# One core, two transformer blocks in fp32: hand-over between projections in units of two k-tiles, one chain for two norms, context rows made between matmul steps

## The chip, the cores and the metric

The kernel runs on one core of one Trainium2 chip. The metric is device microseconds of one execution; the median of three runs is given. The engines are PE (TensorE), ACT (ScalarE), DVE (VectorE), POOL (GpSimd) and SP (SyncE), each with an instruction queue of its own; SP and POOL issue the large transfers. Semaphores order them: an engine that waits holds back everything behind in its queue.

## The reference

256 tokens of width 2048 go through two blocks. Block one: RMS norm, input projection (2048 to 4368), sliding-window attention with sinks and forgetting attention (16 heads each), a norm of each half, output projection; then `x = x + rmsnorm(mix)`, norm, up projection (2 x 5632), a causal depthwise convolution of width 3, `gelu(gate) * val`, down projection, `x = x + rmsnorm(y)`. Block two gets x and a context of 256 rows. Its modulation columns come from `silu(c) @ w_ada + b_ada`.

```
h  = modulate(rms_norm(x, norm_attn_w), sh_a, sc_a)
hc = modulate(rms_norm(ctx, norm_attn_w), csh_a, csc_a)
q, k, v, u = split_projection(h @ w_in); qc, kc, vc, uc = split_projection(hc @ w_in)
x = x + g_a * (concat([attn, pool]) @ w_out)
x = x + g_m * squared_relu_mlp(modulate(rms_norm(x, norm_mlp_w), sh_m, sc_m), w_up, w_down)
return rms_norm(x, final_norm_w)
```

## The kernel before

**Steps.** Every projection is cut into chunks of 512 output columns, and a chunk into steps of two k-tiles (8 steps for a depth of 2048, 6 for the shorter third group of the down projection). fp32 weights and activations are each split into a high part (fp32r) and a low part; PE computes high x high, low x high, high x low for two token blocks and two k-tiles, so a step is 12 matmuls of 128x512 (L1362 to L1364). SP loads raw weights into four slots of two steps. For each step ACT copies `raw` to `w_hi` (`hi`, L541) and DVE subtracts to `w_lo` (`lo`, L837). There are four w buffers, and `hi(s)` waits until step s-4 is done:

```
if s >= 4:
    act.wait_ge(step_done, s - 3 + d)
```

The bodies of a chunk starting at step s prepare the weights of steps s+3 to s+10, so of the next projection the first three steps' weights are ready when a projection ends; the fourth step's come first in ACT's and DVE's next body.

**Projections in order** (names of the code): in1 (9 chunks), attention, out1 (4), up1a/down1a, up1b/down1b, up1c/down1c, in2 (5 chunks, of which the third runs for x and for the context, H + A), attention, pooling and a small mixing matmul (`pool_w`), out2 (4), mlp2 (4 groups of 4 up and 4 down chunks).

**Preparing activations** (`prep` on ACT and DVE, `turn_prep` on PE). Between projections the rows are normalized, transposed and split. Before, this goes in four groups of four k-tiles. PE transposes 8 blocks of 128x128 into two banks of T (L1396). ACT and DVE each take two of the four k-tiles through gain and shift into `u_buf` or `conv` (L521 or L523; L904 or L906). ACT copies 1024 columns to `h_hi` (L531), and DVE subtracts for `h_lo` (L913). All transposes stand ahead of the first step in PE's queue. `h_ready` counts finished groups, and a step waits for its own. The rows are scaled by ACT (token block 0, L502) and DVE (block 1, L886) in pieces of 512 columns.

**Norms.** ACT squares with a running sum (L491), DVE reduces, ACT takes the square root (L497), DVE the reciprocal (L880). After down1c: y2's norm, then x is updated (L1080), then squared, then in2's norm.

**Context.** POOL loads the context into y when in2's activations are ready (L447). ACT squares it after chunk 0 of in2, and the whole preparation stands between chunk 1 and chunk 2.

**Modulation work.** In the gaps of DVE run `ada` operations on tiles of `w_ada` (512 KB each, two buffers) that POOL loads (L402); `ADA_RUNS` is the table of which run does which tiles. A run's loads stand in POOL's queue among its other work: the row for the output scaling (L418), x loaded again (L436, 2 MB), memset of y (L438, L464).

Of the kernel before, what the change touches and what calls it, by code (L numbers as in the profile page):

```python
# [105 lines left out]
def build(nc, a):  # L106
# [173 lines left out]
    PREP = {"in1": (0, 4), "out1": (4, 4), "up1": (8, 4), "in2": (12, 4), "ctx": (16, 4), "out2": (20, 2), "up2": (22, 4)}  # L280
    NORMED = {"out1": 0, "in2": 4, "ctx": 8, "up2": 12}
    X_NEW = {"up1": 0, "in2": 4, "out2": 8, "final": 12}
    STAT = {"in1": 0, "out1": 1, "y1": 2, "up1": 3, "y2": 4, "in2": 5, "ctx": 6, "up2": 7, "final": 8}

    SQUARED = {"in1": 8, "out1": 16, "y1": 24, "up1": 32, "y2": 40, "in2": 48, "ctx": 56, "up2": 64, "final": 72}

    def pipeline(n, pre, gain, fin):

        for t in range(n + 2):
            if t < n and pre:  # L290
                pre(t)
            if 1 <= t <= n:
                gain(t - 1)
            if t >= 2:
                fin(t - 2)
# [1448 lines left out]
```

## Time and profile before

| | us |
|---|---|
| median of three runs (2282.51 to 2287.75) | 2283.95 |
| the profiled execution's own time | 2282.68 |
| its span, first to last instruction | 2281.0 |
| PE busy (share of the span) | 2179.1 (96%) |
| DVE busy | 1526.8 (67%) |
| ACT busy | 1066.0 (47%) |
| POOL busy | 125.7 (6%) |
| mean granted PE clock, 1 is full | 0.976 |

PE is busy nearly always; a share of idle time is not seen in an average, so the places where one projection hands over to the next have to be looked at one by one. Matmuls overlap and their ends are modelled: the time of a step is read from start to start.

### The profile page before, as it was taken

Reading aid. Unit: us, or ns where it says so; the run is one execution under the profiler, and the core shown is the slowest. Engines: PE = TensorE matmul, PEld = TensorE weight load, DVE = VectorE, ACT = ScalarE, POOL = GpSimd, SP = SyncE. Lnnn points to the kernel's source line nnn. Section 1 sums busy time; section 2 is a strip of 40 time slices with the busy share of each in tenths; the row PEclk is TensorE's granted clock in tenths of the full one; section 3 lists DMA queues with packets and bytes.
Section 4 is the critical chain, followed back from the end, with each engine's and each line's share of the span. In section 5 each row is a group of like instructions: output and inputs, shape, how many; then the busy total and the mean of one; then the engine's idle time right before and its main releaser. Section 6 shows DMA issues by size and latency. Waiting matters only on the chain.

```text
span 2281.0 us, 30329 instructions
## 1 busy us (share of the span) xinstructions
PE 2179.1 (96%) x10231; PEld 1803.7 (79%) x10231; DVE 1526.8 (67%) x1841; ACT 1066.0 (47%) x1375; POOL 125.7 (6%) x220
## 2 busy tenths in 40 slices
PE   7999988899999999999978999889999999999997
PEld 5888777788878888888867777777888888888876
DVE  6887778688885787767765364556655555655655
ACT  5444654555433554345456355345434434444442
POOL 1001000100010100100000000001000000000000
PEclk9999999999999999999999999999999999999999
DMA  7886058588786888977645250465656756666652
GB/s 264 293 284 227 1 197 300 192 277 268 267 279 211 275 277 270 299 253 249 221 149 183 87 185 1 148 202 200 224 188 212 239 192 214 232 199 204 223 182 93
DMA packets 267277, 482.50 MB, mean 212 GB/s; under 512 B 15180, under 2 KB 107604, under 8 KB 265888
## 3 DMA queue, kind: packets, MB, share of 16 engines
q1 hardware_dynamic: 236544, 367.18, 48.2%
q0 software_dynamic: 29808, 113.63, 15.8%
q8 instruction: 79, 1.29, 0.2%
q10 hardware_dynamic: 816, 0.16, 0.0%
q14 instruction: 30, 0.25, 0.0%
HBM read 478.80 MB, written 2.11 MB: 211 GB/s over the span
## 4 chain that ended last, share of the span: by engine, by line
PE 92%; ACT 3%; DVE 2%; issue 1%; DMA 1%; ACTq 0%; SPq 0%; DVEq 0%; POOLq 0%; POOL 0%
PE G L1362 28%; PE G L1364 27%; PE G L1363 27%; PE T L1537 1%; PE T L1407 1%; PE T L1646 1%; PE T L1478 1%; PE T L1396 1%; ACT junk L491 1%; PE G L1626 1%; DMA x<-in_x 1%; PE G L1471 1%; PE T L1501 0%; ACT h_hi L531 0%; DMA raw<-in_w_in 0%
## 5 line engine op out<-in xcount | busy, mean ns | idle before, releaser
L837 DVE TENSOR_TENSOR w_lo<-raw,w_hi 128x1024 fp32r<-128x1024 f32 x696 | 844.7, 1223 | 481.7 <-ACT w_hi L541 477.1
L541 ACT ACTIVATE w_hi<-raw 128x1024 fp32r<-128x1024 f32 x696 | 735.8, 1060 | 922.8 <-PE G L1364 921.5
L1362 PE MATMUL G<-w_hi,h_hi 128*128 128x512 f32 (+1 forms) x1920 | 753.2, 392 | 14.5 <-ACT w_hi L541 6.4
L1363 PE MATMUL G<-w_lo,h_hi 128*128 128x512 f32 (+1 forms) x1920 | 748.3, 390 | 0.0
L1364 PE MATMUL G<-w_hi,h_lo 128*128 128x512 f32 (+1 forms) x1920 | 748.2, 390 | 0.0
L1362 PEld LDWEIGHTS G<-w_hi,h_hi 128*128 128x128 f32 x1920 | 363.2, 189 | 91.2 <-issue 9.5
L1364 PEld LDWEIGHTS G<-w_hi,h_lo 128*128 128x128 f32 x1920 | 362.9, 189 | 75.0
L1363 PEld LDWEIGHTS G<-w_lo,h_hi 128*128 128x128 f32 x1920 | 363.1, 189 | 72.9
L1362 PE MATMUL G<-w_hi,a_hi 128*128 128x512 f32 x896 | 353.4, 394 | 3.6 <-issue 1.9
L1364 PE MATMUL G<-w_hi,a_lo 128*128 128x512 f32 x896 | 351.1, 392 | 0.0
L1363 PE MATMUL G<-w_lo,a_hi 128*128 128x512 f32 x896 | 351.0, 392 | 0.0
L1362 PEld LDWEIGHTS G<-w_hi,a_hi 128*128 128x128 f32 x896 | 169.8, 189 | 41.7 <-issue 4.7
L1364 PEld LDWEIGHTS G<-w_hi,a_lo 128*128 128x128 f32 x896 | 169.4, 189 | 35.7
L1363 PEld LDWEIGHTS G<-w_lo,a_hi 128*128 128x128 f32 x896 | 169.6, 189 | 35.4 <-issue 0.5
L402 POOL DMA_DIRECT2D ada_w<-in_w_ada x192 | 101.7, 530 | 1470.7 <-DVE ada_acc L855 897.5
L855 DVE SCALAR_TENSOR_TENSOR ada_acc<-ada_w,silu,ada_acc 128x1024 f32<-128x1024 f32 x122 | 153.6, 1279 | 30.2 <-DMA ada_w<-in_w_ada 30.2
L855 DVE SCALAR_TENSOR_TENSOR ada_third<-ada_w,silu,ada_third 128x1024 f32<-128x1024 f32 x60 | 76.9, 1282 | 59.0 <-DMA ada_w<-in_w_ada 59.0
L945 DVE SCALAR_TENSOR_TENSOR ada_acc<-ada_w,silu,ada_acc 128x1024 f32<-128x1024 f32 x64 | 79.2, 1279 | 0.0
L1113 DVE SCALAR_TENSOR_TENSOR conv<-T,convw,conv 128x255 f32<-128x255 f32 (+1 forms) x176 | 72.6, 475 | 7.8 <-ACT conv L677 5.5
L1396 PE MATMUL T<-consts,y 128*128 128x128 f32 x96 | 19.0, 372 | 30.4 <-ACT y L502 24.0
L1136 DVE TENSOR_TENSOR y<-y,G 128x512 f32<-128x512 f32 x56 | 35.9, 683 | 16.8 <-PE G L1364 16.7
L564 ACT ACTIVATE u_buf<-G,rstdx 128x512 f32<-128x512 f32 x44 | 27.9, 686 | 36.1 <-PE G L1364 36.1
(216 smaller groups left out, 1167.0 us busy)
## 6 DMA issues: line engine op xcount, KB each, us to landing
ada_w<-in_w_ada POOLq DMA_DIRECT2D x192, 512.0 KB, 4.9
raw<-in_w_up SPq DMA_DIRECT2D x176, 512.0 KB, 5.9
raw<-in_w_mlp_up SPq DMA_DIRECT2D x128, 512.0 KB, 4.7
raw<-in_w_mlp_down SPq DMA_DIRECT2D x128, 512.0 KB, 4.7
raw<-in_w_in SPq DMA_DIRECT2D x104, 512.0 KB, 4.8
raw<-in_w_down SPq DMA_DIRECT2D x88, 512.0 KB, 6.0
raw<-in_w_out SPq DMA_DIRECT2D x64, 512.0 KB, 5.1
raw<-in_w_in SPq DMA_DIRECT2D x8, 272.0 KB, 4.0
```

Of the source, the lines that this page charges most:

```text
L402: pool.dma_start(ada_tiles(run)[:, half, :], w_ada[:, bass.ds(t + first // 2, 1), part * D + half * ADA_HALF:part * D + (half + 1) * ADA_HALF]
L541: act.activation(w_hi[:, s % 4], raw[:, s // 2 % 4, STEPK * (s % 2):STEPK * (s % 2) + STEPK, :], ACT.Copy).then_inc(hi_ready, 1)
L564: act.activation(dst(b), G[:, 2 * parity + b, 0:width], func, scale=scale).then_inc(bank_evac, 1)
L837: dve.tensor_tensor(w_lo[:, s % 4], raw[:, s // 2 % 4, STEPK * (s % 2):STEPK * (s % 2) + STEPK, :], w_hi[:, s % 4].bitcast(F32), ALU.subtr ...
L855: ins = dve.scalar_tensor_tensor(out=acc[:, half, :], in0=ada_tiles(run)[:, half, :], scalar=silu[:, c, bass.ds(dt + (first + k) // 2, 1)] ...
L945: ins = dve.scalar_tensor_tensor(out=ada_acc[:, c, half, :], in0=ada_w[:, half, :], scalar=silu[:, c, bass.ds(i * 2 + k // 4, 1)], in1=ada ...
L1113: ins = dve.scalar_tensor_tensor(out=conv[:, j, k:TOK], in0=tt(0)[:, j, 0:TOK - k], scalar=convw[:, tap, bass.ds(t + dt, 1)], in1=conv[:, ...
L1136: dve.tensor_tensor(y[:, b, c * N:c * N + N], y[:, b, c * N:c * N + N], G[:, 2 * (c % 2) + b, :], ALU.add).then_inc(bank_evac, 1)
L1362: pe.matmul(out, ah, wh, start=f, stop=False)
L1363: pe.matmul(out, ah, wl, start=False, stop=False)
L1364: mm = pe.matmul(out, al, wh, start=False, stop=l)
L1396: mm = pe.transpose(tt(g % 2)[:, j, b * P:b * P + P], src[:, b, (4 * g + j) * P:(4 * g + j + 1) * P], ident)
```

## The change

- **Units.** Preparation goes in eight units of two k-tiles, one bank of T each. ACT's `high` makes `h_hi` straight from the bank with the gain, DVE's `low` makes `h_lo` from the bank in one operation each k-tile. With a shift (in2, ctx, up2), `high_shifted` does both k-tiles on ACT (gain and shift into `conv`, then a copy to `h_hi`).
- **Begun between.** PE transposes two units, runs step 0, transposes two, runs step 1, and so on: `begin` for up1, in2 and up2, the like for in1, out1 (four units, three steps, four units) and out2 (three steps among the mixing matmuls, which are now units 4 to 7 and take their gain in `high` and `low`).
- **One chain** behind down1c. The sum of squares of `x + r*z` is worked out as xx + 2r(x.z) + r*r(z.z), with a multiply-and-reduce on DVE (`cross`) and squares of z on ACT, so x is updated by units after both norms.
- **Context** rows are squared inside chunk 0 of in2 and transposed one unit ahead of each step of chunk 1.
- **out1's norm** in two halves, the first while attention ends. ada run (2, 0, 16) becomes (2, 0, 2), inside attention, and (2, 2, 14), inside out1; POOL loads x again ahead of the second. `row` for out2 is loaded when unit 7 of out2 is ready.
- **Start.** x is loaded without waiting for the small vectors, which POOL now issues; pre_mix_g comes alone first.
- The Sqrt table is loaded ahead (`sqrt_table`), in up2 both blocks of rows are scaled by DVE.

```
-ADA_RUNS = ((0, 0, 32), (2, 0, 16), (1, 0, 32), ...
+ADA_RUNS = ((0, 0, 32), (2, 0, 2), (2, 2, 14), (1, 0, 32), ...
 pool:
+        ada(1)
         pool.wait_ge(o_evac, 16)
         load_row(a["post_mix_g"])
-        ada(1)
-        pool.wait_ge(prep_turned, PREP["out1"][0] + 4)
+        pool.wait_ge(prep_turned, PREP["out1"] + UNITS)
         pool.dma_start(x[:], tokens(a["x"])).then_inc(x_again, 16)
+        ada(2)
...
-        pool.wait_ge(mixed_lo, 8)
+        pool.wait_ge(h_ready, PREP["out2"] + UNITS)
         load_row(ada_rows[0:1, :])
...
-        pool.wait_ge(prep_turned, PREP["up2"][0] + 4)
+        pool.wait_ge(prep_turned, PREP["up2"] + UNITS)
         pool.memset(y[:], 0.0).then_inc(y_zero, 1)
         ada(ADA_LAST)
 act:
+        def high_shifted(name, q, gain, shift, hi):
+            act.wait_ge(prep_turned, PREP[name] + q + 1)
+            if q >= 2:
+                act.wait_ge(h_ready, PREP[name] + q - 1)
+            for j in range(2):
+                k = 2 * q + j
+                ins = act.activation(split_tmp(q)[:, TOK * j:TOK * j + TOK], bank(q)[...], ACT.Identity,
+                                     scale=gain[:, k:k + 1], bias=shift[:, k:k + 1])
+            ins.then_inc(tmp_act, 1)
+            act.wait_ge(tmp_act, SHIFTED[name] + q + 1)
+            act.activation(pair_of(hi, q), split_tmp(q), ACT.Copy).then_inc(prep_hi, 1)
...
+            if k == 0:
+                his(s0 + 3, 4)
+                act.wait_ge(ctx_in, 16)
+                for g in range(4):
+                    squares(g, lambda b: y[:, b, g * N:g * N + N])
+                    his(s0 + 7 + g, 1)
+                root("ctx")
+            elif k == 1:
+                for q in range(UNITS):
+                    high_shifted("ctx", q, comb, adac[:, 6, :], a_hi)
+                    his(s0 + 11 + q, 1)
 dve:
+            if j in (10, 12):
+                ada_op(1, j // 2 - 5)
...
-                if k % 2:
-                    ada_op(1, 4 * c + k // 2)
+                if k % 2 and 4 * c + k // 2 < 14:
+                    ada_op(2, 4 * c + k // 2)
...
-        los(s0 + 3, 16)
-        root("ctx", rstd)
+        los(s0 + 3, 8)
+        root("ctx", rstd[:, 0:NB])
 pe:
+        def begin(name, src, s, parity, ready):
+            turns(name, src, 0, 2)
+            for k in range(3):
+                steps(s, k, k + 1, parity, H, ready)
+                turns(name, src, 2 * k + 2, 2 * k + 4)
...
-        turn_prep("ctx", y)
+        for q in range(UNITS):
+            turn("ctx", y, q)
+            step(s0 + 8 + q, 1, H, STEPK * q, q == 0, q == 7, None)
```

ACT ahead of mlp2, before: the last two groups of activations (`u_buf`, `conv`), then the first weight tile of the new projection that isn't ready yet (L541).

```order
L523 ACTIVATE u_buf<-T,adac,comb 128x256 [waits h_ready,prep_turned]
L523 ACTIVATE u_buf<-T,adac,comb 128x256
L531 ACTIVATE h_hi<-conv 128x1024 [waits tmp_dve,tmp_act]
L523 ACTIVATE conv<-T,adac,comb 128x256 [waits h_ready,prep_turned]
L523 ACTIVATE conv<-T,adac,comb 128x256
L531 ACTIVATE h_hi<-u_buf 128x1024 [waits tmp_dve,tmp_act]
L531 ACTIVATE h_hi<-conv 128x1024 [waits tmp_dve,tmp_act]
```

The same place in the change: units 6 and 7 of `high_shifted`, then the fourth step's weights.

```order
L546 ACTIVATE conv<-T,adac,comb 128x256 [waits h_ready,prep_turned]
L546 ACTIVATE conv<-T,adac,comb 128x256
L550 ACTIVATE h_hi<-conv 128x512 [waits tmp_act]
L546 ACTIVATE conv<-T,adac,comb 128x256 [waits h_ready,prep_turned]
L546 ACTIVATE conv<-T,adac,comb 128x256
L550 ACTIVATE h_hi<-conv 128x512 [waits tmp_act]
L912 UNCONDITIONAL_BRANCH
L912 ISA
L558 ACTIVATE w_hi<-raw 128x1024 [waits step_done]
```

The weights of step 3 stand behind the last unit in both; in the change that unit's transposes stand behind step 2 on PE.

POOL around out1, before: the row, the loop of ada loads, then x.

```order
L418 DMA row<-in_post_mix_g 128x2048 [waits squared,o_evac]
L413 UNCONDITIONAL_BRANCH
L413 ISA
L402 ISA [waits ada_used]
L402 DMA ada_w<-in_w_ada 128x1024
L401 REGISTER_ALU
L402 ISA [waits ada_used]
L402 DMA ada_w<-in_w_ada 128x1024
L413 REGISTER_ALU
L413 COMPARE_AND_BRANCH
L436 DMA x<-in_x 128x2x2048 [waits prep_turned]
```

POOL around out1 in the change: x now stands ahead of the loop of ada loads.

```order
L444 DMA row<-in_post_mix_g 128x2048 [waits squared,o_evac]
L462 DMA x<-in_x 128x2x2048 [waits prep_turned]
L439 UNCONDITIONAL_BRANCH
L439 ISA
L428 ISA [waits ada_used]
L428 DMA ada_w<-in_w_ada 128x1024
```

The 2 MB of x moved from behind the ada tiles of out1 to ahead of them, on the same queue.

DVE at the start of out1 in the change: the first ada operation of the run stands ahead of the third weight tile.

```order
L932 TENSOR_TENSOR w_lo<-raw,w_hi 128x1024 [waits hi_ready,row_full]
L932 TENSOR_TENSOR w_lo<-raw,w_hi 128x1024 [waits hi_ready]
L950 SCALAR_TENSOR_TENSOR ada_acc<-ada_w,silu,ada_acc 128x1024 [waits ada_used,ada_full0]
L950 SCALAR_TENSOR_TENSOR ada_acc<-ada_w,silu,ada_acc 128x1024
L932 TENSOR_TENSOR w_lo<-raw,w_hi 128x1024 [waits hi_ready] x2
```

Before, the first ada operation stood at the same place of this queue; what moved is when its tile is asked for.

## Rows read from the trace of the kernel before

**Rows 1.** The page: busy time of each engine over the span.

```profile
PE 2179.1 (96%) x10231; PEld 1803.7 (79%) x10231; DVE 1526.8 (67%) x1841; ACT 1066.0 (47%) x1375; POOL 125.7 (6%) x220
```

**Rows 2.** Waits of the PE: line, for whom, us in total, times, longest.

```profile
PE T L1396 <- ACT y L502: 24.0, 3, 14.7
```

**Rows 3.** PE busy, six stretches: length, busy us (count), clock, DMA share, GB/s.

```profile
0.00:203.40 203.40, 186.64 (x801) 0.98 0.81 272
290.60:390.60 100.00, 93.45 (x417) 0.97 0.79 260
390.60:439.70 49.10, 35.70 (x153) 0.86 0.59 195
1184.80:1263.10 78.30, 56.23 (x259) 0.87 0.39 142
1427.80:1533.00 105.20, 97.86 (x432) 0.98 0.53 173
1533.00:1576.80 43.80, 34.29 (x153) 0.88 0.54 186
```

**Rows 4.** PE timeline, first steps of the first up projection: start, us, instruction.

```profile
413.07 0.39 PE L1362 MATMUL G<-w_hi,h_hi 128*128 128x512 f32 x1
415.79 0.39 PE L1362 MATMUL G<-w_hi,h_hi 128*128 128x512 f32 x1
```

**Rows 5.** PE alone just after an idle stretch: length, busy us, PEclk.

```profile
29.50:34.80 5.30, 5.24 (x13) 0.51 0.62 199
```

**Rows 6.** ACT and PE timelines ahead of the second network's MLP: start, us, instruction.

```profile
1537.26 1.28 ACT L497 ACT_TABLE_LOAD   x1
...
1548.93 0.78 PE L1362 MATMUL G<-w_hi,h_hi 128*128 128x512 f32 x1
```

**Rows 7.** POOL and DVE timelines, same place.

```profile
1549.34 3.53 POOL L464 MEMSET y<- 128x4096 f32 x1 [12.23 <-PE T L1396]
1552.80 1.05 POOL L402 DMA_DIRECT2D ada_w<-in_w_ada  x2
...
1557.04 1.28 DVE L855 SCALAR_TENSOR_TENSOR ada_acc<-ada_w,silu,ada_acc 128x1024 f32<-128x1024 f32 x1 [1.28 <-DMA ada_w<-in_w_ada]
```

**Rows 8.** Single instructions by line: duration min/median/max in ns, first and last start.

```profile
L521 ACT ACTIVATE u_buf<-T,gains x12: 453/462/473, 14.2 to 409.1; 128x256 f32<-128x256 f32 x12
L523 ACT ACTIVATE u_buf<-T,adac,comb x12: 554/561/563, 1201.8 to 1547.4; 128x256 f32<-128x256 f32 x12
L683 ACT ACTIVATE conv<-conv x22: 632/633/636, 446.5 to 1124.7; 128x512 f32<-128x512 f32 x22
L491 ACT ACTIVATE junk<-x x40: 613/630/634, 9.0 to 2270.6; 128x512 f32<-128x512 f32 x40
L1250 DVE CUSTOM_DVE_ANT_0 sm<-G,tab,nsink x32: 745/749/752, 1358.7 to 1412.6; 128x512 f32<-128x512 f32 x32
L853 DVE TENSOR_SCALAR ada_acc<-ada_w,silu x6: 746/748/749, 311.7 to 904.6; 128x1024 f32<-128x1024 f32 x6
```

**Rows 9.** The page: the two halves of splitting a weight tile, mean ns of one.

```profile
L837 DVE TENSOR_TENSOR w_lo<-raw,w_hi 128x1024 fp32r<-128x1024 f32 x696 | 844.7, 1223 | 481.7 <-ACT w_hi L541 477.1
L541 ACT ACTIVATE w_hi<-raw 128x1024 fp32r<-128x1024 f32 x696 | 735.8, 1060 | 922.8 <-PE G L1364 921.5
```

**Rows 10.** DMA issues: queue, count, size of each, us from issue to landing.

```profile
ada_w<-in_w_ada POOLq DMA_DIRECT2D x192, 512.0 KB, 4.9
x<-in_x POOLq DMA_DIRECT2D x1, 2048.0 KB, 12.6
y<-in_ctx POOLq DMA_DIRECT2D x1, 2048.0 KB, 10.4
pool_a<-in_pool_table POOLq DMA_DIRECT2D x1, 1024.0 KB, 5.2
pool_w<-in_pool_w POOLq DMA_DIRECT2D x1, 1024.0 KB, 7.6
row<-ada_rows POOLq DMA_DIRECT2D x1, 1024.0 KB, 5.0
```

More of the change, by code:

```diff
@@ L278, in build, with bank, split_tmp, pair_of @@
     C_C, C_CTX, PRE_MIX, GRP, PRE_FFN, NORM_A, NORM_M, POOL_S = [16 * i for i in range(8)]
[L280 to L295, printed above, removed]
+    PREP = {"in1": 0, "out1": 8, "up1": 16, "in2": 24, "ctx": 32, "out2": 40, "up2": 48}
+    NORMED = {"out1": 0, "in2": 8, "ctx": 16, "up2": 24}
+    SHIFTED = {"in2": 0, "ctx": 8, "up2": 16}
+    X_NEW = {"up1": 0, "in2": 8, "out2": 16, "final": 21}
+    STAT = {"in1": 0, "out1a": 1, "out1b": 2, "y1": 3, "up1": 4, "y2": 5, "in2": 6, "ctx": 7, "up2": 8, "final": 9}
+    SQUARED = {"in1": 8, "out1a": 12, "out1b": 16, "y1": 24, "up1": 32, "y2": 46, "in2": 48, "ctx": 56, "up2": 64, "final": 72}
+    UNITS = 8
+    UCOLS = 2 * P
+    def bank(q):
+        return T[:, q % 4, :]
+    def split_tmp(q):
+        return conv[:, 2 * (q % 2):2 * (q % 2) + 2, :].rearrange("p a b -> p (a b)")
+    def pair_of(t, q):
+        return t[:, 2 * q:2 * q + 2, :].rearrange("p a b -> p (a b)")
     def twice(src, n):
@@ L345, in _ @@
         l0 = FIRST_LOAD["in1"]
-        chunk(l0, w_in1, 0)
+        x_piece(0)
+        x_piece(1)
+        for k in range(4):
+            load(l0 + k, w_in1[:, LOADK * k:LOADK * k + LOADK, 0:N])
+            if k < 2:
+                x_piece(k + 2)
         with sp.Fori(0, 7) as i:
@@ L649, in _ @@
             act.wait_ge(step_done, s0 + 8 * c + 8)
-            squares(c, lambda b: G[:, 2 * (c % 2) + b, :])
+            for b in range(NB):
+                if c == 3 and b:
+                    act.wait_ge(bank_evac, FIRST_EVAC["up1a"] - 1)
+                act.wait_ge(squared, taken[0])
+                act.activation(junk[:], G[:, 2 * (c % 2) + b, :], ACT.Square, accum_out=sq[:, b, c:c + 1]).then_inc(squared, 1)
+                taken[0] += 1
         root("y1")
@@ L780, in _ @@
                            ACT.Copy).then_inc(pooled_ev, 1)
-        prep("out2", None, h_hi)
+        sqrt_table()
+        for q in range(4):
+            high("out2", q, None, h_hi)
+        for q in range(4, UNITS):
+            high("out2", q, gains[:, POOL_S:], h_hi, 8)
         s0 = 2 * FIRST_LOAD["out2"]
@@ L788, in _ @@
                 new_squares("out2")(c - 1)
-        new_squares("out2")(3)
+        for b in range(NB):
+            act.wait_ge(x_new, X_NEW["out2"] + 3 + b + 1)
+            act.wait_ge(squared, taken[0])
+            act.activation(junk[:], x[:, b, 3 * N:4 * N], ACT.Square, accum_out=sq[:, b, 3:4]).then_inc(squared, 1)
+            taken[0] += 1
         root("up2")
-        prep("up2", comb, h_hi, adac[:, 3, :], scale_rows("up2", x, y))
+        for q in range(UNITS):
+            high_shifted("up2", q, comb, adac[:, 3, :], h_hi)
         s0, u0 = 2 * FIRST_LOAD["mlp2"], UP0["mlp2"]
@@ L949, in _ @@
                     dve.wait_ge(ada_used, i * 4 + k // 2 + 1)
+        in1_body(first=True)
+        root("in1", rstdx[:])
+        with dve.Fori(1, 8) as i:
+            in1_body(i)
         los(s0 + 67, 8)
@@ L1154, in _ @@
             if g == "a":
+                root("up1", rstdx[:], keep=xx[:])
+                link(dve.tensor_scalar(xx[:], xx[:], D * EPS, None, ALU.add))
                 dve.wait_ge(y_zero, 1)
```

627 lines of the change are left out of this document (375 added, 252 removed).

## The prediction, made before the changed kernel ran

> **What bounds the kernel now.** I read the page first. PE is busy 96% of the span [rows 1], so a gain can only come from PE's gaps. The waits of PE say where they are: its longest in sum are transposes of L1396 waiting for rows that ACT has scaled [rows 2], the preparation between projections. The shares hide that, so I cut the span at the hand-overs and take from each stretch the matmul steps in it. A step is 12 matmuls; two step starts lie 2.72 us apart [rows 4]. What is left of a stretch is what the hand-over costs PE, transposes included [rows 3]:
> A, start: 203.4 less 64 steps (174.1) = 29.3. B, attention's end to out1's end: 100.0 less 32 steps (87.0) = 13.0. C, out1 to up1: 49.1 less 10 steps = 21.9. D, down1c to the context's steps: 78.3 less 16 steps (43.5) = 34.8. E, pooling's end to out2's end: 105.2 less 32 = 18.2. F, out2 to mlp2: 43.8 less 10 = 16.6. Together 133.8 us. The rest of the span I leave as it is.
>
> **What every hand-over gets.** Gained: step 0 needs one unit instead of a group. Lost: ACT does more, and the order of three queues makes a new wait. The weights of the first three steps are ready beforehand, the fourth's are not; ACT and DVE make them behind unit 7, and PE transposes unit 7 behind step 2. From the end of step 2: four transposes 0.5; ACT's units 6 and 7; then `w_hi` 1.06 and `w_lo` 1.22 [rows 9] with 0.1 of hand-over. A unit without shift is two reads of 0.46 [rows 8], overlapped 0.84. One with shift is two of 0.56 and a copy of 512 columns, taken as the 0.63 of L683 [rows 8]: 1.6 with overlaps and its own wait. So step 3 starts 4.6 us (no shift) or 6.1 us (shift) after step 2, where PE has 0.9 of work. Before, ACT was through with the groups by then. The six units' transposes behind the first two cost 1.8 up to step 2.
>
> PE's clock: after an idle stretch PE ran at 0.51 of full for 5.3 us [rows 5], the 1.2 GHz level, which costs up to 2.6. I charge 2.0 where PE is idle over 4 us and then does only eight transposes; bounds 0 and 2.6.
>
> The Trainium skill ("TensorE: Matmul & The Clock Gate", What's actually happening) says that the ramp is under 1% of a typical span and is not to be fitted. Left out everywhere (A 2, D 3.5, E 2.4, F 2), my sum would be about 2284, no change. The 0.51 of rows 5 speaks for charging it.
>
> **F, worked in full**, from the last matmul of out2. DVE's two blocks of y and x, 0.7 each op: 3.0. Square, 0.63 [rows 8] and the read of its sum, by 3.8; sums, root and reciprocal 1.0: 4.8. The table load that stood there, 1.28 [rows 6], is gone but was partly beside DVE. Scaling unit 0: 0.55. Four slow transposes 1.0, high_shifted 1.6, low 0.7: step 0 at 8.7, where it was 15.9 [rows 6]. Three steps 8.2, transposes 1.8, clock 2.0, then 6.1: step 3 at 26.8. Next is late: POOL's memset of y waits for the last transposes (21.6), takes 3.5, and DVE had its ada tile 4.2 after the load's issue [rows 7]. That makes 29.3, and `lo` of the fifth step is behind the ada operation: 1.28 and 1.22, step 4 at 31.7. Cost 31.7 less 4 steps = 20.8. Before 16.6: **+4.2**. Bounds +2 (no clock loss) and +5.
>
> **C.** The norm of y1 is through 2.8 after the last matmul (blocks done crosswise), residual 0.75, transposes 1.0, unit 0.84 and 0.9: step 0 at 6.5. Its x is loaded long before. x_new 8 at 19.3; memset and load as in F, tile at 27.0, first use 0.75 [rows 8], `lo` 1.22: step 4 at 29.0. The third ada tile is asked for at the first use and takes 0.5 and 4.9 [rows 10] and a hand-over: about 33.7, then 1.28 and 1.22: step 6 at 36.2. Cost 36.2 less 16.3 = 19.9: **-2.0**, bounds -7 (tiles sooner) and 0.
>
> **B.** Two ada operations go into attention, each two of 0.75 [rows 8] on DVE ahead of a copy PE waits for; some 0.5 is slack, so 0.9 each, 1.8 (bounds 0 and 2.8). Step 0 comes 4.3 after the last attention matmul, step 3 by 18.6 (four units behind step 2), with attention's 1.8 at 20.4. But POOL now asks for x, 2 MB, when the last unit is transposed (17.8), and for the ada tile behind it. How this queue serves two requests is in the pair of pool tables: 1 MB in 5.2 and the next, asked for 0.5 later, in 7.6 [rows 10], so one after the other, 2 MB in 8.1 and 2.5 MB in some 9.7. The tile is there at about 28. DVE stands at the ada operation (two of 1.28), with `lo` of step 5 behind: 31.7. Cost with attention: 31.7 less 13.6 = 18.1, less what overlaps the attention's delay 0.6: 17.5, **+4.5**. Bounds: the tile not behind x, 12.2, or -0.8; x at its loaded 12.6 [rows 10], +8.
>
> **D.** Behind down1c DVE has: add to y (1.5), y times row (1.2), two `cross` (0.75 by L1250 [rows 8], 0.8 with the read of the sum), the last y part times row twice 0.7, two `cross`: 7.4. Two norms on sums, 2.8 with their square roots: 10.2. Residual and scaling 1.3, transposes 1.0, unit 1.6 and 0.7: step 0 at 14.9, so that the longest single wait, 14.7 [rows 2], gets shorter by a good half. Then 8.2, 1.8, 2.0 and 6.1: step 3 at 33.0. All units are ready at 31.7 and the context's load begins; it took 10.4 [rows 10]: 42.1. **What is queued behind that wait** is step 7's weights, on ACT; each pair of squares is 1.5 with 1.06 of weights: 10.2. Then `lo` 1.2, root 1.0, gain and scaling 1.0: the first context unit at 55.4, while step 7 was through by 48. Chunk 1 is 21.8 and 32 transposes 3.7 and clock 1.5: 82.4; the evacuation of chunk 1, covered before by the context's transposes, is now bare: 1.2. 83.6 less 43.5 = 40.1, **+5.3**. Bounds: load in 8 and no clock loss, -1; the issue 2.7 late, +8.
>
> **E.** Pooled copy 0.6, table load and root 1.5, high 0.6, low 0.7: step 0 at 3.5; three steps 8.2 and four mixing units of 0.9: 15.3; last high and low 1.8: 17.1. Only now POOL asks for `row`, 5.0 [rows 10], and DVE waits for it ahead of step 3's `lo`: 23.4 less 8.2 = 15.2, clock 2.4: 17.6, **-0.6**. Bounds -3 and +2.
>
> ScalarE's page in the Trainium skill ("ScalarE: Activation LUTs", What ACT_TABLE_LOAD costs) has 1.28 for the load and 1.38 more for a drain. With that E would be 1.4 later. In [rows 6] the load is 1.28 alone, and I found no drain behind it, so I take none.
>
> **A.** x comes sooner and step 0 at about 13, but steps 2 and 3 wait for the later pieces, and the silu columns (a chain PE, DVE, ACT, DVE) and an ada operation stand ahead of step 5's `lo`: step 5 at 42.4 by the same durations, less 13.6 = 28.8: **-0.5**, bounds -5 and +4.
>
> **Sum.** -0.5 + 4.5 - 2.0 + 5.3 - 0.6 + 4.2 = +10.9 on the execution's own 2282.7: 2293.6. The median of before is 1.3 higher than that execution, less than it varies, and isn't added.
>
> **The rivals.**
> 1. *The fourth step's wait is not there or covered* (ACT gets through the units sooner, PE never stands): then each hand-over costs what step 0 and the transposes cost. For: step 0 comes 7 to 8 us sooner in F and D. Against: the queue orders. Without that wait and what is behind it the costs would be B 8, C 11, D 23, E 7, F 13, some 42 us less, 2241; with half of that 2262. Chance 0.15.
> 2. *Gains and losses cancel*: the tile isn't behind x (-5), clock losses small (-4), context in 8 us (-2). 2283. Chance 0.15.
> 3. *The forecast*, 2283 to 2300 with its bounds, chance 0.60, of which 0.57 are beyond the limit of slower.
> 4. *Worse*: the POOL queue late everywhere (x at 12.6, context's issue late, ada tiles behind each other). It decides if the first ada tile of out1 is there later than 12 us after x is asked for. B +8, D +8, with the rest 2300 to 2306. Chance 0.10.
>
> **How the numbers follow.** A measurement of this kernel tells 0.2%, 4.6 us, from no change. Faster: rival 1 and a little of rival 2, 0.18. Same: most of rival 2 and the edge of the forecast, 0.15. Slower 0.67. The range reaches down to 2274, where rival 1 begins to be left out, and up to 2304; 0.13 below and 0.05 above are left out.
>
> **What would show it.** Step 0 of mlp2 some 9 us after out2 and step 3 about 6 us after step 2, PE waiting for `w_lo`; in out1 DVE waiting for `ada_w`; ACT waiting for the context's load inside in2's first chunk; the memset of y in PE's chain before mlp2. Wrong if PE runs from step 2 to step 3 without a wait, or if out1 has no wait for `ada_w`.

## The result and the profile after

| | before | changed |
|---|---|---|
| time, median (runs) | 2283.23 us (4, 2282.04 to 2287.75) | 2306.32 us (4, 2302.37 to 2309.20) |
| profiled execution | 2282.68 us | 2302.37 us |
| its span | 2281.0 us | 2300.7 us |

The ratio is 1.0094, 95% interval 1.0077 to 1.0111: slower by 0.9%, some 22 us. The forecast was 2293.6, with a range of 2274 to 2304. The direction was right, the size was half of what came, and 2306.3 lies above the range. The profiled execution is 19.7 us longer in span; where those are is the question.

The page of the changed kernel answers [rows 1]: PE is busy 4 us longer and the span is 19.7 longer, so most of it is PE standing.

```profile
PE 2183.2 (95%) x10232; PEld 1799.9 (78%) x10232; DVE 1518.3 (66%) x1897; ACT 1074.6 (47%) x1432; POOL 134.8 (6%) x233
```

PE's waits, in the same form as [rows 2] (for whom, us in total, times, longest). The 14.7 us of the second norm are now 10.9, but there are ten waits for `w_hi`, 28.8 us, where before there were four, 7.8 us (last row), and the row "issue" (11 times, 8.7 the longest) hides another.

```profile
PE G L1532 <- ACT w_hi L558: 28.8, 10, 5.1
PE G L1532 <- issue: 16.7, 11, 8.7
PE T L1563 <- ACT y L524: 15.6, 5, 10.9
PE T L1563 <- DVE y L981: 11.8, 3, 6.5
...
PE G L1362 <- ACT w_hi L541: 7.8, 4, 3.9
```

PE busy in the stretches that answer to [rows 3], A to F in order (length, busy us and count, clock, DMA share, GB/s):

```profile
0.00:204.10 204.10, 184.01 (x802) 0.98 0.81 271
289.60:391.60 102.00, 94.29 (x417) 0.97 0.78 262
391.60:438.50 46.90, 37.06 (x153) 0.89 0.50 165
1184.10:1273.60 89.50, 62.37 (x257) 0.81 0.34 118
1436.60:1544.70 108.10, 97.61 (x433) 0.97 0.52 170
1544.70:1596.60 51.90, 37.55 (x153) 0.84 0.46 155
```

Less the same steps of 2.72 us these cost 30.0, 15.0, 19.7, 46.0, 21.1 and 24.7. A sharper ruler is the start of the same step in two traces: the n-th of the 704 groups of four matmuls of `w_hi` with `h_hi` or `a_hi`, which are the same in every kernel here. Its shift against before, taken at the boundaries, gives each stretch's change without a choice of windows, and the experiments are read by it. The same code differs from one profile to another by about 1 us or less in D, E and F, by 2 in B and C, by 3 in the first MLP, and by 4 to 5 in the start, of which more below.

| stretch (steps) | forecast | measured |
|---|---|---|
| A, start to attention (0 to 71) | -0.5 | +0.7 |
| B, attention and out1 (to 103) | +4.5 | +0.3 |
| C, up1's hand-over (to 113) | -2.0 | -2.2 |
| first network's MLP (to 367) | 0 | +0.3 |
| D, in2 with the context (to 386) | +5.3 | +9.7 |
| E, pooling and out2 (415 to 447) | -0.6 | +2.9 |
| F, mlp2's hand-over (to 460) | +4.2 | +8.0 |

**F in rows.** The timelines of PE, DVE and POOL behind out2's end at 1544.9 (start, us, instruction, idle before):

```profile
1547.58 2.03 DVE L1333 TENSOR_SCALAR comb<-adac 128x16 f32<-128x16 f32 x1
...
1573.34 1.23 DVE L932 TENSOR_TENSOR w_lo<-raw,w_hi 128x1024 fp32r<-128x1024 f32 x1 [0.26 <-ACT w_hi L558]
1577.69 1.28 DVE L950 SCALAR_TENSOR_TENSOR ada_acc<-ada_w,silu,ada_acc 128x1024 f32<-128x1024 f32 x1 [3.13 <-DMA ada_w<-in_w_ada]
...
1547.75 1.82 POOL L489 MEMSET ada_acc<- 128x2048 f32 x1
1569.60 3.52 POOL L491 MEMSET y<- 128x4096 f32 x1 [20.03 <-PE T L1563]
1573.06 1.05 POOL L428 DMA_DIRECT2D ada_w<-in_w_ada  x2
...
1555.06 0.76 PE L1532 MATMUL G<-w_hi,h_hi 128*128 128x512 f32 x1 [1.74 <-DVE h_lo L1001]
...
1560.79 0.48 PE L1532 MATMUL G<-w_hi,h_hi 128*128 128x512 f32 x1
...
1568.46 1.08 PE L1563 MATMUL T<-consts,y 128*128 128x128 f32 x8
1574.66 0.76 PE L1532 MATMUL G<-w_hi,h_hi 128*128 128x512 f32 x1 [5.12 <-ACT w_hi L558]
...
1580.22 0.48 PE L1532 MATMUL G<-w_hi,h_hi 128*128 128x512 f32 x1
```

Step 0 comes at 1555.06, 10.2 behind out2, where it was 15.9 [rows 6]. Then PE is through with step 2 and the last two units' transposes at 1569.5 and stands 5.12 us for the fourth step's weights. The profile puts this wait down to `w_hi`; by the times the low part ends last, at 1574.57 (1573.34 and 1.23), 0.09 ahead of step 3. This is the mechanism of the prediction, and its price (6.1 from the end of step 2 to step 3; 6.2 in the trace). DVE then waits 3.13 us for the gate tile (a tile of `w_ada`; a gate operation is an ada operation on it), as forecast, and step 4 starts 5.56 behind step 3. But PE doesn't stand there: step 3 itself takes that long, at half clock. This step and the same one in out1 (length, PE busy, clock, DMA share, GB/s):

```profile
1574.66:1580.22 5.56, 5.46 (x13) 0.51 0.94 340
307.87:313.12 5.25, 5.25 (x13) 0.50 0.99 400
```

**D in rows.** DVE and ACT while in2's units are made:

```profile
1206.69 0.69 DVE L1001 TENSOR_TENSOR h_lo<-conv,h_hi 128x512 fp32r<-128x512 f32 x1 [3.21 <-ACT h_hi L550]
1207.30 0.87 DVE L1198 SCALAR_TENSOR_TENSOR x<-y,rstd,x 128x256 f32<-128x256 f32 x2
1208.21 0.35 DVE L981 TENSOR_SCALAR y<-x,rstdx 128x256 f32<-128x256 f32 x1
1210.32 0.69 DVE L1001 TENSOR_TENSOR h_lo<-conv,h_hi 128x512 fp32r<-128x512 f32 x1 [1.76 <-ACT h_hi L550]
...
1208.21 0.51 ACT L524 ACTIVATE y<-x,rstdx 128x256 f32<-128x256 f32 x1 [1.55 <-DVE x L1198]
1208.62 1.00 ACT L546 ACTIVATE conv<-T,adac,comb 128x256 f32<-128x256 f32 x2
1209.66 0.63 ACT L550 ACTIVATE h_hi<-conv 128x512 fp32r<-128x512 f32 x1
```

The two engines wait for each other in turn: `h_lo` of unit q, residual and row scaling of unit q+2 (DVE), then ScalarE's scaling of its block (`y`, L524), which stands in its queue ahead of the reads of unit q+1, then `h_hi`, then `h_lo` of q+1. From 1206.69 to 1210.32 that is 3.63 us for each unit, and PE waits for the rows. The experiments call this the ring.

**E and B in rows.** Mixing units on PE, the load of `row` on POOL and DVE's wait for it; then, in out1, the request for x and DVE's wait for the gate tile behind it:

```profile
1442.95 1.89 PE L1859 MATMUL T<-pooled,pool_w 128*128 128x256 f32 x8
...
1464.22 0.77 PE L1532 MATMUL G<-w_hi,h_hi 128*128 128x512 f32 x1 [8.73 <-issue]
...
1457.85 0.54 POOL L444 DMA_DIRECT2D row<-ada_rows  x1 [88.54 <-DVE h_lo L993]
...
1462.89 2.36 DVE L932 TENSOR_TENSOR w_lo<-raw,w_hi 128x1024 fp32r<-128x1024 f32 x2 [5.62 <-DMA row<-ada_rows]
...
304.03 0.73 POOL L462 DMA_DIRECT2D x<-in_x  x1 [8.34 <-PE T L1563]
...
314.24 2.48 DVE L950 SCALAR_TENSOR_TENSOR ada_acc<-ada_w,silu,ada_acc 128x1024 f32<-128x1024 f32 x2 [5.34 <-DMA ada_w<-in_w_ada]
```

### The profile page after: what moved, and what is told of

It is laid out like the page before. It is cut to its first block, busy times and chain, and to the rows that moved or that the text cites. A ratio compares the mean times of both kernels' runs of the same rounds, so it can differ in the third digit from the quotient of the medians.

```text
span 2300.7 us, 30219 instructions
## 1 busy us (share of the span) xinstructions
PE 2183.2 (95%) x10232; PEld 1799.9 (78%) x10232; DVE 1518.3 (66%) x1897; ACT 1074.6 (47%) x1432; POOL 134.8 (6%) x233
## 3 DMA queue, kind: packets, MB, share of 16 engines
q0 software_dynamic: 30192, 113.72, 15.5%
## 4 chain that ended last, share of the span: by engine, by line
PE 92%; ACT 4%; DVE 2%; issue 1%; DMA 1%; ACTq 0%; DVEq 0%
PE G L1532 28%; PE G L1534 27%; PE G L1533 27%; PE T L1723 1%; PE T L1834 1%; PE T L1585 1%; PE T L1663 1%; ACT w_hi L558 1%; PE G L1814 1%; PE T L1563 1%; ACT conv L546 1%; PE G L1656 1%; ACT junk L508 0%; ACT h_hi L535 0%; DMA y<-in_ctx 0%
## 5 line engine op out<-in xcount | busy, mean ns | idle before, releaser
L1532 PE MATMUL G<-w_hi,h_hi 128*128 128x512 f32 (+1 forms) x1920 | 762.8, 397 | 53.0 <-ACT w_hi L558 25.9
L734 ACT ACTIVATE conv<-T,convw 128x256 f32<-128x256 f32 x88 | 42.4, 563 | 0.8
```

The lines of the kernel that those rows point to most:

```text
L734: ins = act.activation(conv[:, j, :], tt(0)[:, j, :], ACT.Identity, scale=convw[:, 2, bass.ds(t + dt, 1)], bias=convw[:, 3, bass.ds(t + dt ...
L1532: pe.matmul(out, ah, wh, start=f, stop=False)
```

## The experiments

All start from the changed kernel. The table gives the shift against before by stretch, in us, from each kernel's profiled execution, and the median and ratio of its runs. The stretches are those of the table above; MLP is the first network's.

| kernel | A | B | C | MLP | D | E | F | total | median, ratio [95%] |
|---|---|---|---|---|---|---|---|---|---|
| the change | +0.7 | +0.3 | -2.2 | +0.3 | +9.7 | +2.9 | +8.0 | +19.7 | 2306.3, 1.0094 [1.0077, 1.0111] |
| w4_early | +4.5 | +3.5 | -0.6 | -1.0 | +12.8 | +0.1 | +9.1 | +27.7 | 2311.0, 1.0117 [1.0100, 1.0134] |
| in2_rows_dve | +4.8 | -0.6 | -0.8 | -1.2 | +4.1 | +2.9 | +7.8 | +16.5 | 2304.2, 1.0095 [1.0075, 1.0114] |
| row_at_attention | +0.6 | 0.0 | -2.6 | 0.0 | +9.9 | -1.2 | +8.8 | +14.8 | 2297.2, 1.0057 [1.0039, 1.0076] |
| zeros_early | +4.9 | -0.3 | -1.6 | -2.9 | +9.8 | +2.6 | +6.9 | +18.8 | 2302.6, 1.0085 [1.0068, 1.0102] |
| gates_later | +4.0 | -1.9 | -2.7 | +2.4 | +9.9 | +2.4 | +7.9 | +21.8 | 2306.3, 1.0092 [1.0059, 1.0126] |
| w4_gates_later | +5.4 | -4.5 | -6.4 | +6.2 | +12.6 | +0.5 | +2.3 | +15.5 | 2298.8, 1.0055 [1.0037, 1.0072] |
| all_w4 | +4.7 | -4.4 | -6.6 | +8.1 | +3.6 | -6.8 | +1.8 | -0.2 | 2281.4, 0.9979 [0.9965, 0.9994] |
| all_w5 | +5.2 | -4.6 | -7.1 | +2.2 | +3.7 | -7.6 | -1.3 | -10.1 | 2277.9, 0.9974 [0.9961, 0.9987] |
| start_weights | -6.7 | +1.6 | -1.6 | +0.3 | +9.9 | +2.7 | +7.7 | +13.6 | 2297.6, 1.0062 [1.0046, 1.0079] |
| one_unit_a_step | +1.6 | -6.0 | -10.6 | +7.4 | +4.4 | -7.6 | -1.8 | -13.1 | 2269.2, 0.9931 [0.9912, 0.9949] |
| one_unit_context_later | +1.5 | -6.0 | -10.5 | +7.5 | -7.9 | -7.6 | -1.8 | -23.2 | 2258.8, 0.9888 [0.9872, 0.9904] |
| one_unit_final | -2.1 | -7.9 | -10.0 | +5.0 | -6.0 | -7.6 | -2.8 | -29.9 | 2253.8, 0.9856 [0.9832, 0.9881] |

(What is left between the columns and the total, 1.6 at most, lies in the second attention and behind step 460.)

**w4_early: the fourth step's weights ahead of the last two units.**

```diff
 for q in range(UNITS):
+    if q == 6:
+        his(2 * FIRST_LOAD["mlp2"] + 3, 1)
     high_shifted("up2", q, comb, adac[:, 3, :], h_hi)
```

The same on VectorE, and in out1, up1, in2 and out2.

> The changed kernel, with the fourth step's weights of out1, up1, in2, out2 and mlp2 made by ScalarE and VectorE ahead of the last two units instead of behind them. Theory 1 (the prediction's: the wait behind step 2 is for these weights alone, because they stand behind unit 7 in both queues): in each of the five hand-overs step 3 starts right behind step 2, and what is late next is step 4, whose weights come where step 3's came. One step, 2.7 us, is gained in out1, up1, out2 and mlp2; in in2 nothing, since the units and the context's load come no sooner there. Together -11 us, 2291 to 2292 for the profiled execution. Theory 2 (the step 3 wait is the engines' total work on units and weights, whatever the order): step 4 waits longer by what step 3 no longer waits, 0, 2302 to 2306.

Its profiled execution became 8 us slower, 4 of them in the start, which it doesn't touch (the clock, below); the medians differ by 4.7. PE's and DVE's waits in F (1540 to 1600), each from its own answer:

```profile
PE G L1557 <- issue: 7.2, 2, 6.7
...
DVE ada_acc L961 <- DMA ada_w<-in_w_ada: 4.2, 1, 4.2
```

And the timelines of POOL and DVE there:

```profile
1576.86 3.53 POOL L491 MEMSET y<- 128x4096 f32 x1 [19.87 <-PE T L1588]
1580.34 1.05 POOL L428 DMA_DIRECT2D ada_w<-in_w_ada  x2
...
1584.53 1.29 DVE L961 SCALAR_TENSOR_TENSOR ada_acc<-ada_w,silu,ada_acc 128x1024 f32<-128x1024 f32 x1 [4.19 <-DMA ada_w<-in_w_ada]
1585.73 1.22 DVE L943 TENSOR_TENSOR w_lo<-raw,w_hi 128x1024 fp32r<-128x1024 f32 x1
```

Step 3 came with 0.5 us of the wait left, but step 4 stood 6.7 us: DVE had the first gate operation ahead of the fourth low part that was left, and its tile is asked for behind POOL's fill of y. So there are two waits at one place, and removing one uncovers the other. In F the clock still falls twice, now behind step 4's wait instead of step 3's; in out1 it falls once more (steps 3 and 5 take 4.4 and 5.2 us, where the change had 5.3 and 2.8), and B is 3.2 worse. Theory 1 is right that step 3 waited for the queue order, and wrong on what is late next. The wait for the fourth step's weights was real, and removing it alone gained nothing in out1, up1, in2 and mlp2; in out2 it gained 2.8.

**gates_later and w4_gates_later: the gate operations later, without and with the weights.**

```diff
-                if k % 2 and 4 * c + k // 2 < 14:
-                    ada_op(2, 4 * c + k // 2)
+                if k % 2 and 4 * c + k // 2 >= 2:
+                    ada_op(2, 4 * c + k // 2 - 2)
```

In up1 and mlp2 the first chunk's gate operations begin at the fifth low part; mlp2's wait for the zeros goes with them.

> The changed kernel, with VectorE's gate operations of the first chunk of out1, up1 and mlp2 begun later (in out1 two places later, in up1 and mlp2 from the fifth low part on, in mlp2 with the wait for the zeros); weights in their old order. Theory 1 (step 3 waits for its weights, made behind unit 7; step 4 and 5 then wait for a gate tile, since the gate operation stands ahead of their low part): step 3's waits stay (4.1, 3.4, 5.1 us), those behind go: 1.6 in out1 and the delay of step 4 there, 1.3 in up1, 2.8 in mlp2. -5 us, 2297 to 2298. Theory 2 (the tile alone sets the pace): also step 3's waits shrink. Theory 3 (the engines' total work): 0 to -1.

> The changed kernel, with the fourth step's weights ahead of the last two units as in w4_early, and the gate operations later as in gates_later. w4_early became slower: step 3 came 1.5 to 4.8 us sooner, but step 4 up to 4.2 later than that, with VectorE standing at the gate tile ahead of step 4's low part. Theory 1 (two waits in a row, weights and then gate tile, each hiding the other): now both go, out1, up1 and mlp2 gain 4 to 6 each, out2 2.7, in2 nothing: 2284 to 2288 for the profiled execution. Theory 2 (total work of the engines): no better than gates_later, 2297 or more.

F settles it: +8.0 in the change, +9.1 with the weights early, +7.9 with the gates late, +2.3 with both. Neither alone is worth anything, together 5.7. With the gates late alone, step 3 of mlp2 still takes 5.3 us at half clock: the tile's wait had been covered by that slow step. C reads the same way (-2.2, -0.6, -2.7, -6.4). In B (+0.3, +3.5, -1.9, -4.5) the gates late gain 2.2 by themselves, since there the tile's wait came one step later, behind the slow step. gates_later missed its forecast (2297 to 2298; its profiled execution took 2304.4, with the start 3.3 longer than the change's), and so did both together (2284 to 2288; 2298.2). In up1 a new wait took its place, 6 us in the column MLP: four gate operations, one behind each low part, now stand ahead of the norm that the first chunk's evacuation needs.

**in2_rows_dve: the ring in in2.** ScalarE's `in2_scale` goes, VectorE scales both blocks:

```diff
-        in2_scale = scale_rows(x, y, lambda q, b: rstdx[:, b:b + 1])
+        in2_scale = scale_rows(x, y, lambda q, b: rstdx[:, b:b + 1], (0, 1))
```

> The changed kernel, with in2's rows of both token blocks scaled by VectorE, as up2 has it, so that ScalarE only makes the units. Theory 1 (in in2 the two engines wait for each other in turn: h_lo of unit q, residual and scaling of q+2, ScalarE's scaling of q+2, high part of q+1, h_lo of q+1, 3.63 us a unit in the trace): the ring is gone, a unit takes VectorE's own 2.1 us, unit 7 is ready about 8 us sooner, the context's load is issued 8 us sooner, and the stretch from down1c's end to the context's double steps is 7 to 8 us shorter: 2294 to 2296 for the profiled execution. Theory 2 (the units come late because of ScalarE's three instructions a unit, as the prediction had it): ScalarE saves 0.5 a unit, 3 to 4 us. Theory 3 (weights and slow clock set in2's pace): 0 to 1 us.

D fell from +9.7 to +4.1, 5.6 us, though VectorE has more work and ScalarE 0.5 less a unit. Two units now lie 2.05 apart where they don't wait for PE, instead of 3.63:

```profile
1208.59 0.69 DVE L991 TENSOR_TENSOR h_lo<-conv,h_hi 128x512 fp32r<-128x512 f32 x1 [3.56 <-ACT h_hi L550]
1209.20 0.88 DVE L1188 SCALAR_TENSOR_TENSOR x<-y,rstd,x 128x256 f32<-128x256 f32 x2
1210.11 0.62 DVE L971 TENSOR_SCALAR y<-x,rstdx 128x256 f32<-128x256 f32 x2
1210.64 0.68 DVE L991 TENSOR_TENSOR h_lo<-conv,h_hi 128x512 fp32r<-128x512 f32 x1
```

Theory 1, a little short of its 7 to 8, since PE stands at the fourth step's weights after all (4.2 us). Four other profiles of kernels with the ring and the old order of weights have +9.8 or +9.9 in D, so the 5.6 is clear of noise. The runs' times don't show it: A is 4.1 worse in its profile, its four runs go from 2299.2 to 2309.9, and the ratio is that of the change.

**row_at_attention.** `load_row(ada_rows[0:1, :])` one line up, ahead of the wait for the last mixing unit.

> The changed kernel, with the load of the gate row for out2 asked for when the second attention's last output is written, instead of when the last mixing unit is ready; nothing else in the queue moves. Theory 1 (step 3 of out2 waits for this load, issued late because the unit's readiness comes behind step 2): the row is there 20 us ahead, VectorE makes the fourth step's low part as soon as ScalarE has the high part, step 3 starts about 5.6 us sooner, 2296.7 for the profiled execution. Theory 2 (the weights bind anyway): less than 1 us.

E went from +2.9 to -1.2, 4.1 us of the 5.6 expected; the load is asked for at 1430.11, 28 us sooner. Step 3 still waits 3.3 us for the weights. With w4 as well (all_w4) E is at -6.8: again two waits at one place, 4.1 and 2.8 alone, 9.7 together.

**zeros_early.** `pool.memset(ada_acc5[:], 0.0)` behind the load of `final_row`, during out2, instead of at its end.

> The changed kernel, with GpSimd's fill of the second gate accumulator done during out2 instead of at out2's end. In the trace VectorE's 128x16 operation for the modulation column takes 2.03 us there (0.17 elsewhere) and ends 0.04 after the fill. Theory 1 (VectorE's small operation is held by the fill, and it is in the chain to mlp2's step 0): it takes 0.17, step 0 comes 1.5 to 1.8 us sooner, and steps 3 and 4 too: -1.5, 2300.8 for the profiled execution. Theory 2 (the 2.03 is another wait, or the first gate tile sets step 4 anyway): 0.

The same DVE instruction in that kernel:

```profile
1548.26 0.17 DVE L1333 TENSOR_SCALAR comb<-adac 128x16 f32<-128x16 f32 x1
...
1549.20 0.16 DVE L970 TENSOR_REDUCE ssq<-sq 128x2 f32<-128x8 f32 x1 [0.56 <-ACT junk L882]
```

It takes 0.17 where the change had 2.03, so the fill had held it. ScalarE's last square is the next in that chain, 0.56 later. From the last step of out2 to step 0 of mlp2 it is 11.73 us instead of 13.06, a gain of 1.3, where six other kernels with the fill at its old place have 13.06 or 13.07. F gained 1.1, which alone would be no more than its noise.

**all_w4 and all_w5: the parts together.** w4_gates_later, in2_rows_dve, row_at_attention, zeros_early, and the context's load on `prep_turned` instead of `h_ready`; in all_w5 `his(..., 2)` at the same places.

> w4_gates_later with in2's rows by VectorE (measured -6), the gate row loaded at attention's end (-5), GpSimd's zeros early (-1), and the context's load asked for when in2's last unit is transposed instead of when it is ready. If these add up and the context's load is then 2 to 3 us earlier than the chain needs it: 11 to 15 below w4_gates_later, 2270 to 2276, below the kernel before. If the context's load and its squares set the end of in2's first chunk whatever comes ahead, 4 less.

> all_w4 with the fifth step's weights also ahead of the last two units. Theory 1 (queue order): step 4 no longer waits for weights behind unit 7; 1.5 to 2.7 less in each of five hand-overs, up to -10. Theory 2 (the last units are then late instead, step 6 waits): 0, or up to +3.

all_w4 is level with the kernel before (0.2% below by its ratio), and its profiled execution, 2282.5, is 6 above the forecast (the MLP column, up1's new wait). all_w5's profiled execution is 10 us shorter, but it was the fastest of its seven. Of the 10, 5.9 are in the column MLP, 3.1 in F and 0.8 in E; the medians differ by 3.6 and the ratios by 0.0005, so most of the 10 isn't shown. What is clear is that step 4 of mlp2 starts 2.84 behind step 3 instead of 4.60. D stays at +3.7: ScalarE waits 6.2 us for the context there, and the second chunk waits for ScalarE.

**start_weights.** `his(0, 4)` and `los(0, 4)` behind in1's fourth unit.

> The changed kernel, with the weights of in1's third and fourth step made right behind those of the first two, ahead of the units whose pieces of x come later. In the trace of the change PE waits 3.47 us ahead of step 2 and again ahead of step 3, each time for weights made behind two units; and in seven of eight profiles of kernels with this same start PE's clock fell to 1.2 GHz behind the first of these waits, in the change's own not. Theory 1 (order of the queues): both waits go, the clock stays up, step 4 comes at 29 to 30 us instead of 36.7 or 40.8; the start is 7 us shorter than the change's own profile and 11 shorter than the usual: 2291 to 2296. Theory 2 (x's pieces come late): steps 2 and 3 wait as before, 0.

A: -6.7, which is 7.4 below the change's profile. Theory 1; the two waits of 3.47 us are gone, and step 4 comes at 29.4. The clock falls later, behind a wait of 2.1 us ahead of step 5. The profiled execution took 2296.3, the upper edge of the forecast.

**one_unit_a_step, one_unit_context_later, one_unit_final.** The hand-over in another order: one unit behind each step, and each step's weights next to it in both queues; the first two gate tiles asked for ahead of fill and x.

```diff
             turns(name, src, 0, 2)
-            for k in range(3):
+            for k in range(6):
                 steps(s, k, k + 1, parity, H, ready)
-                turns(name, src, 2 * k + 2, 2 * k + 4)
+                turn(name, src, k + 2)
...
         for q in range(UNITS):
+            if q >= 2:
+                hi(2 * FIRST_LOAD["mlp2"] + q + 1)
             high_shifted("up2", q, comb, adac[:, 3, :], h_hi)
```

> All of all_w4's parts; in each hand-over one unit is transposed behind each step instead of two behind each of three, ScalarE and VectorE make one step's weights with each unit (in in1 the first four steps' right away), and GpSimd asks for the first pair of gate tiles ahead of the fill and of x instead of behind them. Theory 1 (each wait so far came from several units in a row ahead of weights that PE wants next): no wait is left after step 0, a hand-over costs what step 0 and 0.44 a unit cost. Against all_w5 (-10 to before): start -9, out1 -3, up1 and what follows -4, in2 -2, out2 -2, mlp2 -3: 2247 to 2257 for the profiled execution. Theory 2 (ScalarE, 1.6 a unit and 1.06 a step's weights, is the bound whatever the order): 2265 to 2272.

> one_unit_a_step, with the context's first unit transposed behind the sixth step of in2's second chunk instead of ahead of its first, three units there and five between the double steps. Theory 1 (PE stands at the second chunk only because the context's load, its squares and norm are queued ahead of it, though that chunk doesn't need them): the wait ahead of the chunk goes, 3 to 6 us less than one_unit_a_step, 2243 to 2253. Theory 2 (the context's chain then makes the double steps wait as long): 0.

> one_unit_context_later, in which two waits are left that its trace names: in in1 PE stands 8.5 us ahead of step 11 (the first chunk's evacuation needs the norm, whose sums VectorE adds up only behind two gate operations that wait for their tiles and ScalarE's two further weights), and in up1 2.7 us ahead of the tenth step and 1.5 behind it (the same, with one gate operation). Here VectorE does the norm ahead of those gate operations and takes them up one by one later. Theory 1 (that order alone makes these waits): step 11 of in1 comes 9 to 10 us sooner and up1's second chunk 1.5 to 2: 2246 to 2248 for the profiled execution. Theory 2 (ScalarE's squares, 6.1 us in either place, bound both): 2254 to 2257.

In mlp2 the steps that carry a unit start 3.2 us apart without a wait: 2.72 and the four transposes, 0.5 (PE in one_unit_context_later; the first row is step 1, then steps 2, 3 and 4):

```profile
1526.95 0.48 PE L1569 MATMUL G<-w_hi,h_hi 128*128 128x512 f32 x1
...
1530.16 0.48 PE L1569 MATMUL G<-w_hi,h_hi 128*128 128x512 f32 x1
...
1533.36 0.47 PE L1569 MATMUL G<-w_hi,h_hi 128*128 128x512 f32 x1
...
1536.57 0.48 PE L1569 MATMUL G<-w_hi,h_hi 128*128 128x512 f32 x1
```

The first of the three missed its forecast: its profiled execution took 2269.6, in the range of theory 2. Against all_w5 it gained 3.6 in the start, 1.4 in out1, 3.5 in up1 and 0.5 in mlp2, nothing in out2, and lost 0.7 in in2 and 5.2 in the first MLP. Not for theory 2's reason, though: between steps that carry a unit PE doesn't wait, but for 0.6 us in out1. all_w5 had already removed most of those waits, and new ones came where the norm's sums queue behind gate operations, 8.3 us ahead of step 11 of in1 and 3.1 in up1. The context behind the sixth step took 12.3 us out of D, where PE had stood 13.8 ahead of the context's first unit, and gave 2.0 back in the second attention. That is more than the 3 to 6 expected: theory 1, though its 2243 to 2253 was built on the forecast before it and was missed (2259.5). The last kernel put those norms first. In1's step 11 came without its wait and A fell by 3.6, not the 9 to 10 expected: in1's step 13 and up1's step 11 then stood up to 4.4 us at the gate operations that had been put off. With 2252.8 for the profiled execution it lies between its theories; in in1 VectorE has 4.8 us of low parts and gate operations for each two steps of 5.4 us, so it catches up by only 0.6 in two steps. Of its four executions one took 4432 us, twice the others (2251.7, 2252.8, 2254.8); nothing here explains that one. one_unit_context_later, with 2256.6 to 2260.0 in four, is the version to take: 1.1% faster than the kernel before.

## Why the prediction was half right

The forecast was +10.9 us, and the profile shows +19.7. By stretch the difference is A +1.2, B -4.2, C -0.2, the first MLP +0.3, D +4.4, E +3.5 and F +3.8. Three terms were too low, and it is luck that B's was too high and that the profiled execution had the short start; without the two the sum would have been further off.

**Right.** That the new cost is the fourth step's weights behind unit 7, with its 6.1 us in F; that VectorE waits for the gate tile next; that the context's load ends in a wait in ScalarE's queue (5.95 us); steps 0 of B, D, E (3.9, 14.8 and 3.5 us behind their starts, forecast 4.3, 14.9, 3.5); C's -2.0 (-2.2, with step 4 at 29.0 as forecast). Of what it named as signs, one didn't come: the memset of y is not in PE's chain before mlp2, which goes through the units, the fourth step's weights and the slow step 3. The first rival, that the fourth step's wait is not there, was wrong of this change; of a schedule without that wait and what is behind it, it said 42 us below before, and one_unit_final reached 30.

**Wrong, by its own steps:**

- *"B: ... two ada operations go into attention ... 1.8"*: 0. From the first softmax transpose to attention's end it is 49.98 us in both traces. "But POOL now asks for x ... (17.8)": at 14.4, since PE's waits there were short (1.3 and 0.6 us) and its clock stayed up. What the queue does was right: x asked for at 304.03, the tile behind it in use at 314.24, 10.2 later (forecast 9.7 and more). B came out 4.2 too high. Of these, 1.7 lie in no term of it: the 64 transposes at attention's start, the same code in both, took 10.81 us before and 9.14 in the change, with the clock at half for 7.6 and 4.2 us of them.
- *"D: ... Then 8.2, 1.8, 2.0 and 6.1: step 3 at 33.0"*: 41.0. The prediction added ScalarE's and VectorE's work for a unit and didn't follow who waits for whom. The scaling of rows queued ahead of a unit's read made a ring of 3.63 us. in2_rows_dve shows 5.6 us of it. The context's load took 8.7 instead of 10.4, which gave some back.
- *"E: ... four mixing units of 0.9: 15.3"*: a mixing unit is eight matmuls of 256 columns, 1.8 us in L1859's rows, so 3.6 are missing, and E's +2.9 against -0.6 is that term. The row for it was in the trace before, 32 such matmuls in 7.18.
- *"F: ... Square, 0.63 and the read of its sum ... step 0 at 8.7"*: 10.2. VectorE's 128x16 operation was held 1.9 by the fill of `ada_acc5`; POOL's queue was read for the tiles but not for what its fill does to VectorE. zeros_early brings step 0 1.3 sooner. Steps 0 to 2 took 1.4 more than forecast, 0.9 of it a wait for scaled rows, and step 3 to step 4 0.7 more; these three make the 3.6 by which step 4 was late (35.3, forecast 31.7).
- *"I charge 2.0 where PE is idle over 4 us"*: once in a hand-over, and not in out1. In up1, in2 and mlp2 there are two such waits, ahead of step 0 and of step 3, and both cost. Step 3 took 4.45 in in2 and 4.33 in out2 (there 2.4 had been charged) instead of 2.72, 1.6 to 1.7 more, and 5.25 in out1 and 5.56 in mlp2, 2.5 and 2.8 more, with the clock at 0.50 and 0.51 and PE busy. In mlp2 the forecast has 4.9 there, for the tile: the size was nearly right and the cause was another.
- *"A: ... steps 2 and 3 wait for the later pieces"* (of x): they waited for weights that stood behind two units in the queues; start_weights moves only those and both waits of 3.47 go. Step 5 came at 42.4 as forecast, and A at +0.7, but that is luck: seven of eight other profiles with the same start show +4.0 to +5.4. The gap between the change's profiled run (2302.4) and its median (2306.3) fits that, though the other runs have no trace to show it.

The page that says the ramp is not to be fitted ("TensorE: Matmul & The Clock Gate", What's actually happening, in the Trainium skill) would have made the forecast 2284. Its "under 1%" is not contradicted: the 9.9 us that the prediction lists for the clock are 0.4% of the span. But they are as large as the change in question, and the rows of steps at 4.3 to 5.6 instead of 2.7 us speak against leaving them out where a change adds waits. The one on the table load ("ScalarE: Activation LUTs", What ACT_TABLE_LOAD costs) would have put E 1.4 later; step 0 of out2 came 3.5 behind pooling's end, as forecast without a drain, and the next instruction starts as the load ends:

```profile
1437.26 1.28 ACT L518 ACT_TABLE_LOAD   x1
1438.55 0.20 ACT L518 ACTIVATE unused<-ones_col 128x1 f32<-128x1 f32 x1
```

## What to carry to other kernels

When a finer grain starts the consumer sooner, write down for each queue what stands between two things that the consumer needs in turn; give each step its weights next to its unit, rather than units in a row and weights behind. Where two waits end at the same place, or a slow step covers the second, an experiment that removes one can show nothing, or a loss: remove both before a theory is dropped. And put what a reduction needs ahead of what only has to be done at some time.

## What was not expected of the hardware

**The same short wait costs the clock in one execution and not in another.** PE waits 3.47 us ahead of step 2 of in1. In the change its clock was full behind it, in zeros_early, with the same code up to there, half (PE over that step: length, busy, clock):

```profile
25.10:28.00 2.90, 2.83 (x12) 1.00 0.66 256
```

```profile
25.50:30.80 5.30, 5.26 (x13) 0.50 0.30 112
```

The step took 2.9 us in the one and 5.3 in the other, at 2.4 and at 1.2 GHz. Of nine profiles with that start two kept the clock there and seven lost it. Some 4 us of this kernel's time hang on that, and start_weights removes the place: its four runs lie within 2.8 us (2296.3 to 2299.0), the change's within 6.8; four runs each are few. The Trainium skill ("TensorE: Matmul & The Clock Gate", What's actually happening) says that the number of slow matmuls at a kernel's start varies from run to run; here the same holds of a wait in the middle.

**A fill on GpSimd holds a small operation on VectorE for its whole length**: 2.03 us instead of 0.17, ending 0.04 behind the fill. So it is in all seven kernels with the fill at that place (2.02 or 2.03), and 0.17 in the six that have it elsewhere. Not every operation is held: `h_lo` ran beside the fill of y (1569.60 to 1573.12, in the rows of F) in its usual 0.69:

```profile
1570.81 0.69 DVE L1001 TENSOR_TENSOR h_lo<-conv,h_hi 128x512 fp32r<-128x512 f32 x1 [1.98 <-ACT h_hi L550]
```

The Trainium skill ("SBUF — State Buffer", SBUF: two separate sides) has the two engines' shared ports as an exclusive lock, held for a whole instruction, which a VectorE operation needs in a two-port mode, or with two SBUF inputs against a GpSimd operation that reads SBUF. Both observations agree with that (`h_lo` has two inputs, and the fill only writes); that the held operation ran in a two-port mode is not shown.
